# A product of two SBUF tiles moves from GpSimd to VectorE in the gated layers of a sparse-expert stage

## The reference

```python
def peer_ffn(x, wq, keys, u_tab, v_tab):
    ...
    expert = i1 * N_KEYS + i2
    gates = jax.nn.softmax(c_score, axis=-1)
    ...
        a = jax.nn.gelu(jnp.einsum('td,thkd->thk', xb, u).astype(jnp.float32), approximate=False)
        w = (gb * a).astype(xb.dtype)
        vv = jnp.take(v_tab, eb, axis=0)
        return jnp.einsum('thk,thkd->td', w, vv)
```

## Time and profile before

| | |
|---|---|
| median of 3 runs | 1709.83 us (1707.11 to 1712.1) |
| profiled execution, its own time | 1707.15 us |
| its span, first to last instruction | 1705.4 us |
| mean granted clock of TensorE | 0.993 |
| busy: PE, DVE, ACT, POOL | 98%, 70%, 55%, 7% |
| the gated steps (all but the first three) | 1134.2 to 1343.3 us of the span |

### The profile page before, as it was taken

One profiled execution on the slowest core, in us unless ns is written; L12 is line 12 of the kernel. 1 busy time (PEld: TensorE's weight loads), 2 busy tenths in 40 slices (PEclk: granted clock), 3 DMA queues, 4 the chain that ended last, 5 costly groups with the idle time before them and its releaser, 6 DMA issues.

```text
span 1705.4 us, 30633 instructions
## 1 busy us (share of the span) xinstructions
PE 1667.1 (98%) x10346; PEld 1476.0 (87%) x10346; DVE 1192.4 (70%) x1845; ACT 938.7 (55%) x1560; POOL 117.6 (7%) x106
## 2 busy tenths in 40 slices
PE   7999999999999999999989999999999999999998
PEld 6888898889897888879889999989999888888887
DVE  5555687597665655567754899989999866666654
ACT  6445546476655544456544444477777654554554
POOL 0000004000000000010010000123233100000000
PEclk9999999999999999999999999999999999999999
DMA  7555563334544655644354546444444366666663
GB/s 264 187 183 184 173 198 124 111 106 135 169 161 147 200 183 172 208 150 162 122 183 142 170 160 209 160 161 148 148 147 142 130 209 194 191 192 195 192 191 122
DMA packets 78814, 286.79 MB, mean 168 GB/s; under 512 B 8864, under 2 KB 9120, under 8 KB 78624
## 3 DMA queue, kind: packets, MB, share of 16 engines
q1 hardware_dynamic: 77888, 282.27, 51.0%
q0 software_dynamic: 864, 3.67, 0.6%
HBM read 284.86 MB, written 1.05 MB: 168 GB/s over the span
## 4 chain that ended last, share of the span: by engine, by line
PE 81%; DVE 9%; issue 6%; ACT 3%; DVEq 1%; ACTq 0%; DMA 0%; POOL 0%; POOLq 0%
PE ps L1777 25%; PE ps L1779 25%; PE ps L1778 25%; DVE one_at_key L1680 3%; DVE w_low L1027 2%; ACT gate_high_at_key L953 1%; PE ps L1792 1%; DVE gate_low_at_key L1697 1%; PE ps L1874 1%; ACT w_high L502 0%; DVE xT_low L1066 0%; PE ps L2310 0%; PE ps L2154 0%; PE ps L2016 0%; PE ps L2034 0%
## 5 line engine op out<-in xcount | busy, mean ns | idle before, releaser
L1027 DVE TENSOR_TENSOR w_low<-ring,w_high 128x1024 fp32r<-128x1024 f32 x532 | 653.8, 1232 | 324.8 <-ACT w_high L502 323.1
L502 ACT ACTIVATE w_high<-ring 128x1024 fp32r<-128x1024 f32 x532 | 559.1, 1055 | 304.6 <-PE ps L1779 297.9
L1777 PE MATMUL ps<-xT_high,w_high 128*128 128x256 f32 x1600 | 460.7, 288 | 2.3 <-DVE xT_low L1066 2.3
L1778 PE MATMUL ps<-xT_high,w_low 128*128 128x256 f32 x1600 | 453.1, 283 | 0.0
L1779 PE MATMUL ps<-xT_low,w_high 128*128 128x256 f32 x1600 | 452.9, 283 | 0.0
L1777 PEld LDWEIGHTS ps<-xT_high,w_high 128*128 128x128 f32 x1600 | 307.0, 192 | 6.4 <-DVE w_low L1027 2.7
L1778 PEld LDWEIGHTS ps<-xT_high,w_low 128*128 128x128 f32 x1600 | 307.3, 192 | 0.7 <-issue 0.5
L1779 PEld LDWEIGHTS ps<-xT_low,w_high 128*128 128x128 f32 x1600 | 307.1, 192 | 0.0
L1777 PE MATMUL ps<-w_high,expert_w_high 128*128 128x512 f32 x512 | 200.4, 391 | 0.0
L1778 PE MATMUL ps<-w_high,expert_w_low 128*128 128x512 f32 x512 | 200.1, 391 | 0.0
L1779 PE MATMUL ps<-w_low,expert_w_high 128*128 128x512 f32 x512 | 200.1, 391 | 0.0
(11 more groups left out here) (378 smaller groups left out, 2113.9 us busy)
## 6 DMA issues: line engine op xcount, KB each, us to landing
ring<-in_stream SPq DMA_DIRECT2D x532, 512.0 KB, 3.7
row_gain<-in_rows POOLq DMA_DIRECT2D x4, 512.0 KB, 4.4
h<-in_x SPq DMA_DIRECT2D x2, 512.0 KB, 5.5
mem_sb<-in_mem SPq DMA_DIRECT2D x1, 1024.0 KB, 10.4
keys_sb<-in_keys POOLq DMA_DIRECT2D x1, 1024.0 KB, 5.1
out<-result SPq DMA_DIRECT2D x2, 512.0 KB, 2.6
last_gain<-in_rows POOLq DMA_DIRECT2D x1, 512.0 KB, 4.8
cols<-in_cols SPq DMA_DIRECT2D x1, 78.5 KB, 3.6
```

The costliest lines, as they stand in the source:

```text
L502: act.activation(WH[:, n % SLOTS, :], RING[:, n % SLOTS, :], ACT.Copy).then_inc(w_high, 1)
L1027: dve.tensor_tensor(WL[:, n % SLOTS, :], RING[:, n % SLOTS, :], WH[:, n % SLOTS, :].bitcast(F32), ALU.subtract).then_inc(w_split, 1)
L1777: pe.matmul(out, high, w_hi, start=start, stop=False, skip_group_check=True)
L1778: pe.matmul(out, low, w_hi, start=False, stop=False, skip_group_check=True)
```

## The change

GpSimd's loop of products is taken out; what is left there is a wait for the last gelu before the DMA of the last gain. VectorE gets the same instruction as `block_weighed`, with the same two waits. In its loop it stands first in the step: block_weighed(q-1), low1(q-2), weigh(q-3), hot2(q-1), split, hot1(q-1); so `low1` also moves ahead of `weigh`. The first product (step 2) stands ahead of weigh(0), the last one (step 63) after the loop. Nothing else is different; lines after L473 have smaller numbers in the changed kernel.

```diff
-        def product(s, dyn=None, late=True):
-
-            pool.wait_ge(gelu_ok, at(STEP0 + s + 1, dyn))
-            if late:
-                pool.wait_ge(weighed, at(s - 2, dyn))
-            n = STEP0 + s
-            slot = GE[:, n, :] if dyn is None else GE[:, bass.ds(dyn + n, 1), :].rearrange("p a t -> p (a t)")
-            pool.tensor_tensor(slot, slot, GELU[:, s % 2, :], ALU.mult).then_inc(prod_ok, 1)
-
-        pool.wait_ge(slots_one, 3)
-        product(2, late=False)
-        product(3)
-        with pool.Fori(1, STEPS // 4) as i:
-            for q in range(4):
-                product(q, i * 4)
+        pool.wait_ge(gelu_ok, EXPERT_BLOCKS)
         pool.dma_start(LAST_GAIN[:], rows[4].partition_broadcast(P)).then_inc(row_in, 16)
...
+        def block_weighed(s, dyn=None, late=True):
+
+
+            dve.wait_ge(gelu_ok, at(STEP0 + s + 1, dyn))
+            if late:
+                dve.wait_ge(weighed, at(s - 2, dyn))
+            n = STEP0 + s
+            slot = GE[:, n, :] if dyn is None else GE[:, bass.ds(dyn + n, 1), :].rearrange("p a t -> p (a t)")
+            dve.tensor_tensor(slot, slot, GELU[:, s % 2, :], ALU.mult).then_inc(prod_ok, 1)
+
...
         dve.wait_ge(gelu_ok, FIRST_GATED)
+        block_weighed(2, late=False)
         dve.wait_ge(prod_ok, 1)
         weigh(0)
         hot2(2)
         hot1(2)
         with dve.Fori(1, STEPS // 4) as i:
             for q in range(4):
+                block_weighed(q - 1, i * 4)
+                low1(q - 2, i * 4)
                 weigh(q - 3, i * 4, 1)
-                low1(q - 2, i * 4)
                 hot2(q - 1, i * 4)
                 split(b + STEP0 + 3 + q, 1, i * 4)
                 hot1(q - 1, i * 4)
+        block_weighed(STEPS - 1)
         low1(STEPS - 2)
```

## The result

| | before | after |
|---|---|---|
| median of 6 runs each, taken in turn on one chip | 1706.97 us (1706.48 to 1712.1) | 1691.3 us (1690.84 to 1699.71) |
| ratio, with its 95% interval | | 0.9912 (0.9894 to 0.993) |
| profiled execution: own time, span | 1707.15, 1705.4 us | 1690.84, 1688.8 us |
| mean granted clock of TensorE | 0.993 | 0.995 |
| one gated step | 3.604 us | 3.387 us |

The change makes the kernel 0.9% faster.

The account below looks back on a forecast made before the run. VectorE was taken to bound the kernel, slowed by GpSimd's product. Gated steps 10.96 us plus stage end 0.91 made 11.9 off 1707.15, 1695.3; with 2.7 added for the median, 1698.0 us, range 1692.5 to 1704.5.

Parts of the forecast that it names:

- TensorE's floor: Gated steps: TensorE's shortest step, 3.38 us plus a quarter of 0.14 for the loop's turn, 3.415 us.
- the clock behind the gap: After TensorE's wait at the stage's end: clock falls to half as before, nothing gained; otherwise 2.4 to 2.9 us.
- the 2.7 us added for the median: Whole kernel: median 1709.83 lay 2.7 us above the profiled 1707.15, so 1695.3 was raised to 1698.0.
- what bounds the kernel: Gated steps: VectorE sets the pace at 3.604 us; GpSimd's product lengthens hot1, costing VectorE 0.58 us a step.
- the product just adds: Rival, gated steps: hot1's length has another cause, so the product adds 0.34 us a step, 1729.5 us; chance 0.06.
- the price of the product on VectorE: Gated steps: the moved 128x256 product takes 0.34 us of VectorE a step, as the low half of the weights.
- VectorE's new step: Gated steps: 3.604 less 0.58 plus 0.34, 3.364 us.
- TensorE becomes the bound: Gated steps: VectorE's step falls 0.05 us under TensorE's 3.415, which becomes the step; 10.96 us gained over 58 steps.
- The gap: Stage's end: TensorE's wait for group 62's gate columns falls from 3.02 to about 2.1 us, gaining 0.91.
- the clock holds: Rival, stage's end: with a gap of 2.1 us or less the clock stays up, 2.9 us less, 1695.1; chance 0.23.
- VectorE's waits on itself: Rival, gated steps: low1 and weigh each lose 0.11 us waiting on VectorE's own results, 1700 to 1708 us; chance 0.24.

Follow-up runs that it names:

- experiment 1: Changed kernel plus an unread GpSimd product, memset or copy of 128x256 in every gated step: 1721.34, 1694.57 and 1703.56 us.
- experiment 2: Changed kernel with VectorE's product made twice, or cut to 16 of 256 columns: 1716.07 and 1696.01 us; steps 3.675 and 3.387 us from 196.42 us window.
- the idle product: Changed kernel plus a GpSimd product per gated step into a spare tile nobody reads: 1721.34 us, ratio 1.0064 to the kernel before.
- the copy: Changed kernel plus a GpSimd copy, one SBUF input, per gated step into a spare tile nobody reads: 1703.56 us, ratio 0.9969 to the kernel before.
- two products: Changed kernel with the product made twice on VectorE, once into a spare tile: 1716.07 us, ratio 1.0033 to the kernel before.
- only low1 moved: Kernel before with low1 put ahead of weigh and the product left on GpSimd: 1721.22 us, ratio 1.0055.
- the two with low1 not moved: Changed kernel with low1 left behind weigh: 1709.97 us; the same with VectorE's gated steps written out instead of looped: 1706.34 us.
- the change again: Changed kernel unaltered, measured once more beside three variants on one chip: 1695.64 us, ratio 0.9909 to the kernel before.
- experiment 5: Changed kernel repeated, with the stage-end gap filled, or lengthened by three or five spare VectorE products: 1695.64, 1694.99, 1698.96, 1701.63 us.

## Where the prediction was right, and where its sum failed

The mechanism was right. What failed is the size of three terms of the sum, all in the same direction: TensorE's floor, the clock behind the gap, and the 2.7 us added for the median.

**Right: what bounds the kernel.** VectorE set the pace, held up by GpSimd's product. Without it hot1 is short, and experiment 1 brings it back with a product that nobody waits for. The rival in which the product just adds (1729.5) is out: it needs a hot1 that keeps its long form, and hot1 is at 416 ns.

**Right: the price of the product on VectorE**, 0.34 from the earlier trace rows: 0.34 from start to start. VectorE's new step was given as 3.364 and is 3.335.

**Right: TensorE becomes the bound** (experiment 2), with room of 0.05, as given.

**Mis-sized: TensorE's floor.** "Its floor is therefore 3.38 + 0.14 / 4 = 3.415". The 0.14 at the turn of the loop was read in a stretch where VectorE set the pace. In the changed kernel the first matmul of a block starts 0.43 to 0.44 behind the gates in all four steps of a turn (1201.36 to 1201.80, and so on), and the step is 3.387, the 3.38 of the earlier trace rows alone. That is 58 x 0.028 = 1.6 us. In the seven profiles in which VectorE sets the pace (the kernel before, the idle product, the copy, two products, only low1 moved, and the two with low1 not moved) 14 of the 58 steps have 0.57 to 0.59 at this place; in the seven in which TensorE does, none has more than 0.44. So the turn costs nothing once the gates never come late; that it is then worked off while matmuls are still queued is my reading and was not tried.

**Mis-sized: the clock behind the gap.** "2.1 lies between, a little nearer to 2.63, so I let the clock fall as before: nothing gained." The gap was right (2.1 foreseen, 2.11 measured), what follows it is not decided by its length alone: with 2.11 to 2.12 us the clock held in two profiles and fell in two. In the profile after it held: 2.43 us for the matmuls, as priced (2.4), and 0.08 for the slow gates ahead of them. Together that is 2.5 and not the 2.9 that the prediction gives (its own two parts, 2.43 and 1.07 - 0.43 = 0.64, add up to 3.07), because the 0.36 us wait for the low half, of which the prediction says nothing, takes up what faster gates give. And a fall of the clock does not cost what it cost in the profile before: in the profile of the change again it fell, and from the gates of step 61 to the thirteenth matmul it took 8.44 us (1334.28 to 1342.72) against 10.40 before and 6.99 where it held, so that even then this end gained 1.96 us, not 0.91. The rival "the clock holds" (1695.1) is what happened in the profile after.

**Mis-sized: the run against which it was summed.** 2.7 us were added since the median of the runs shown lay that far above the profiled execution. Three more runs brought that median to 1706.97, below the profiled 1707.15. With three runs in groups that lie a few us apart, a median is one or the other by chance. Chance is also in the 6.7 us: six more runs of the changed kernel ("the change again" of experiment 5) had a median of 1695.64, inside the range, beside 1710.49 for the kernel before. The gain is the steadier number: 11.8 us forecast, 15.7 and 14.9 measured. The remaining 0.6 us lies before the stage, where the change does nothing. The four together, 1.6 + 2.5 + 0.6 + 2.7, are 7.4. The median after lies 0.5 above its profiled run, and the own times differ by 0.3 less than the spans, so that 6.6 are left, which is the 6.7 missed but for rounding.

**The rival "VectorE's waits on itself"** did not occur, but its mechanism is real and was underpriced. Its chance of 0.24 rested on whether one instruction between is enough; it is, in both places. Had low1 stayed where it was, the rival would have decided, at 0.28 a step.

The Trainium skill's page Perfetto Trace Analysis, section "Optimizing Scalar/DVE Operations", says that with VectorE saturated moving work off it, even to GpSimd, may make sense, and that between these two it might not help because they share a read port. For this product the doubt is right: on GpSimd it costs VectorE 0.58 us a step from start to start, on VectorE its own 0.34.

Still open: what decides whether the clock holds after a wait of 2.1 us, and which of the wait instruction and the register work makes up the 0.1 us of the loop's form.

## What to carry to other kernels

A GpSimd instruction that reads SBUF (here a product, and a plain copy) beside a busy VectorE with two-input instructions is not free even when nobody waits for it: look in the timeline whether a VectorE instruction ends a constant time behind GpSimd's, and compare its length with one where GpSimd is idle. When work is added to a full in-order engine, put an instruction that is needed by nobody next between each pair of producer and consumer; here the move gained nothing without that order (ratio 1.0005 against 0.9912). Take an engine's floor from a stretch in which it never waited, and a clock's behaviour behind a gap from several executions.

## What the runs showed of the hardware that was not expected

The price of needing the result just ahead on the same engine: 0.03 us after the end, so 0.11, for the small pair of the earlier trace rows; 0.19 for a product of 128x256 ahead of weigh with constant waits; 0.28 to 0.31 inside a run-time loop; and 0 with one instruction of 0.34 us between.

An exclusive hold in numbers: hot1 ended 0.27 to 0.28 us behind the end of GpSimd's instruction in the kernel before, with the idle product and with the copy alike, and a copy with a single input did it as well as a product (1.16 us long, hot1 615 ns in the mean).

The granted clock is lower for a few us in early stages that no edit touches, and not for equally long in each execution. Window 802 to 812 us of the profile after, and of the change again:

```profile
802.00:812.00 10.00, 10.00 (x97) 9.43 (x96) 4.96 (x11) 2.60 (x3) 0.00 (x0) 1.00 0.37 128
```

```profile
802.00:812.00 10.00, 10.00 (x78) 9.72 (x76) 6.42 (x15) 2.69 (x4) 0.00 (x0) 0.84 0.32 107
```

TensorE is busy throughout in both. Ahead of this stretch the change again is 1.6 us behind (a split starts at 799.89 and not at 798.28), behind it 3.1 us (the next one starts at 807.20 and not at 804.10). With what other such stretches add (0.83 against 0.66 in the window 250 to 260, for one), the gates of step 3 start at 1133.63 in one and 1137.84 in the other, 4.2 us apart before the changed stage begins. The two spans are 5.7 us apart (1688.8 and 1694.5): these 4.2, and the 1.46 behind the gap of experiment 5.
